# The gated delta stage's decay matrices made from broadcast rows of running sums

## The reference, cut to what matters

```python
dec = jnp.cumsum(g, axis=-1)
gam = jnp.exp(jnp.where(incl, dec[..., :, None] - dec[..., None, :], -jnp.inf))
a_low = jnp.where(strict, jnp.einsum('bhnid,bhnjd->bhnij', kb, k) * gam, 0.0)
t_inv = lax.linalg.triangular_solve(a_low + eye, ...)
qk = jnp.einsum('bhnid,bhnjd->bhnij', q, k) * gam
...
v_new = u_c - jnp.einsum('bhck,bhkv->bhcv', w_c, s)
o = jnp.einsum('bhck,bhkv->bhcv', qd_c, s) + jnp.einsum('bhcs,bhsv->bhcv', qk_c, v_new)
```

## Time and profile before

| | us |
|---|---|
| three runs: lowest, median, highest | 2285.00, 2287.24, 2290.63 |
| the profiled execution, its own time | 2291.59 |
| its span from the first to the last instruction | 2289.8 |
| PE busy / DVE / ACT / POOL in the span | 2212.5 / 1489.2 / 893.0 / 1098.7 |
| gated delta stage, from SP's first issue to the next stage's first matmul | 399.68 to 660.69 |
| start of the four trips' exps (L1128) | 406.29, 468.81, 531.69, 594.55 |

### The profile page before, as it was taken

One profiled execution on the slowest core, in us unless ns is written; L12 is line 12 of the kernel. 1 busy time (PEld: TensorE's weight loads), 2 busy tenths in 40 slices (PEclk: granted clock), 3 DMA queues, 4 the chain that ended last, 5 costly groups with the idle time before them and its releaser, 6 DMA issues.

```text
span 2289.8 us, 30456 instructions
## 1 busy us (share of the span) xinstructions
PE 2212.5 (97%) x10576; PEld 1842.1 (80%) x10576; DVE 1489.2 (65%) x3535; ACT 893.0 (39%) x1420; POOL 1098.7 (48%) x885
## 2 busy tenths in 40 slices
PE   8999868999989999999999999999999999999998
PEld 6787756888878888888888888888888888888886
DVE  4554568666654362078788888893339887878783
ACT  6454354444443333243333333342323323232343
POOL 3433134544424334426666666665427665555500
PEclk9999979999999999999999999999999999999999
DMA  4222143255233232234444444446479999999940
GB/s 171 78 89 74 40 131 107 95 192 192 92 115 129 98 132 89 88 96 142 148 142 148 138 152 145 145 143 245 149 248 342 389 375 364 343 363 345 363 168 37
DMA packets 168815, 403.12 MB, mean 176 GB/s; under 512 B 27648, under 2 KB 101632, under 8 KB 158368
## 3 DMA queue, kind: packets, MB, share of 16 engines
q1 hardware_dynamic: 133920, 334.77, 42.4%
q0 software_dynamic: 34816, 67.41, 8.0%
HBM read 336.84 MB, written 65.28 MB: 176 GB/s over the span
## 4 chain that ended last, share of the span: by engine, by line
PE 68%; DVE 1%; DMA 1%; ACT 1%; issue 0%; POOL 0%; DVEq 0%; POOLq 0%
PE ps L1434 13%; PE ps L181 11%; PE ps L183 11%; PE ps L182 11%; PE ps L2494 7%; PE ps L2495 7%; PE ps L2496 7%; PE ps L1767 1%; PE ps L2546 1%; DMA down_picked_gelu_sb<-a_dense,chosen_gelu_at_sb 0%; DMA a_dense<-up_gelu_sb 0%; POOL down_picked_gelu_sb L2226 0%; PE ps L1517 0%; PE ps L2524 0%; ACT ffn_norm_scaled_sb L1658 0%
## 5 line engine op out<-in xcount | busy, mean ns | idle before, releaser
L2015 POOL DMA_INDIRECT g_dense<-up_gates_summed_sb,up_gate_at_sb x384 | 414.8, 1080 | 259.5 <-issue 216.2
L181 PE MATMUL ps<-n_high_sb,up_u_high_sb 128*128 128x512 f32 x1024 | 398.5, 389 | 0.0
L183 PE MATMUL ps<-n_high_sb,up_u_low_sb 128*128 128x512 f32 x1024 | 398.4, 389 | 0.0
L182 PE MATMUL ps<-n_low_sb,up_u_high_sb 128*128 128x512 f32 x1024 | 398.4, 389 | 0.0
L2494 PE MATMUL ps<-down_v_high_sb,down_w_high_sb 128*128 128x512 f32 x768 | 299.0, 389 | 1.0 <-DVE down_w_low_sb L2270 1.0
L2496 PE MATMUL ps<-down_v_high_sb,down_w_low_sb 128*128 128x512 f32 x768 | 298.8, 389 | 0.0
L2495 PE MATMUL ps<-down_v_low_sb,down_w_high_sb 128*128 128x512 f32 x768 | 298.8, 389 | 0.0
L1858 DVE TENSOR_TENSOR up_u_low_sb<-up_u_sb,up_u_high_sb 128x1024 fp32r<-128x1024 f32 x128 | 156.2, 1222 | 143.7 <-ACT up_u_high_sb L2034 143.2
L2414 ACT ACTIVATE down_v_high_sb<-down_v_sb 128x1024 fp32r<-128x1024 f32 x120 | 125.8, 1048 | 308.8 <-PE ps L2496 292.0
L2236 POOL DMA_INDIRECT expert_rows_sb<-expert_v,chosen_expert_sb x128 | 155.9, 1218 | 167.1 <-DVE h_sb L2286 64.1
L2046 ACT ACTIVATE up_gelu_sb<-ps 128x512 f32<-128x512 f32 x128 | 76.5, 598 | 407.0 <-PE ps L183 406.9
(11 more groups left out here) (366 smaller groups left out, 4524.3 us busy)
## 6 DMA issues: line engine op xcount, KB each, us to landing
up_u_sb<-expert_u SPq DMA_DIRECT2D x128, 512.0 KB, 3.8
down_v_sb<-expert_v SPq DMA_DIRECT2D x32, 2048.0 KB, 11.9
a_dense<-up_gelu_sb SPq DMA_DIRECT2D x128, 256.0 KB, 2.2
g_dense<-nought_sb SPq DMA_DIRECT2D x8, 3072.0 KB, 11.2
down_gelu_sb<-a_dense SPq DMA_DIRECT2D x32, 768.0 KB, 4.7
down_gates_sb<-g_dense SPq DMA_DIRECT2D x32, 768.0 KB, 6.3
w_slots_sb<-w_conv SPq DMA_DIRECT2D x19, 1024.0 KB, 4.8
decay_rows_sb<-decay_sum_rows SPq DMA_DIRECT2D x16, 512.0 KB, 6.0
```

The costliest lines, as they stand in the source:

```text
L181: pe.matmul(out, ah, bh, start=k == 0, stop=False)
L182: pe.matmul(out, ah, bl, start=False, stop=False)
L183: last = pe.matmul(out, al, bh, start=False, stop=k == n - 1)
L2015: pool.indirect_dma_start(cells, at, summed[:, tt, k:k + 1], None).then_inc(stored[tt], 16)
```

## The change

The gated delta stage makes its decays as the SSD stage does. `project_stage` writes all 48 running sums back into `m.decay` (SSD's 32, then the gated delta heads' 8 forward and 8 backward), turns and stores 48 rows, and then makes of each pair the two numbers a token that limits and biases need. `m.sums` is gone, and `m.decay` has two spare columns of zeros. In `gdn_stage`:

- SP loads, for each unit, the rows of forward and backward sums of a head, broadcast over 128 partitions (128 x 2 x 256 fp32, 256 KB): four loads ahead of the halves, and four after every even gate piece, behind a wait for the exps that read the tile.
- DVE makes the log decays (`limits`, two operations of 128x128 a unit). Those of trip one stand ahead of the loop, those of the next trip ahead of z of unit 0. The last trip makes limits that nobody reads.
- ACT takes the exp, two of 128x128 a unit, with a sum as bias: one matrix a chunk, which serves both directions. POOL's masks read it twice.
- TensorE's sums (L1280), POOL's steps (L1181) and the tile `steps` are gone. TensorE begins a trip with the k-k and q-k products, and POOL's mask of a unit waits, besides the exp, for the unit's last output.

```diff
                     sums = m.ps[:, 5, :].rearrange("p (n t a c) -> p n t a c", n=4, t=TT, a=2)
                     for n in range(2):
-                        act.activation(m.sums[:, :, n * SSD_H:(n + 1) * SSD_H], sums[:, n, :, 0, :], ACT.Copy)
+                        act.activation(m.decay[:, :, n * SSD_H:(n + 1) * SSD_H], sums[:, n, :, 0, :], ACT.Copy)
+                        at = 2 * SSD_H + n * GDN_H
+                        act.activation(m.decay[:, :, at:at + GDN_H], sums[:, n, :, 1, n * GDN_H:(n + 1) * GDN_H], ACT.Copy)
...
                         dve.tensor_tensor(w, w, m.small[:, c:TT:TS, c * SSD_H:(c + 1) * SSD_H], ALU.mult)
                 if t == ROWS_AT + 2:
                     dve.wait_ge(rows_turned, 1)
-                    forward, backward = m.sums[:, :, 0:SSD_H], m.sums[:, :, SSD_H:2 * SSD_H]
-                    st.done(dve.tensor_tensor(backward, backward, forward, ALU.subtract))
-                    dve.tensor_scalar(forward, forward, -1.0, None, ALU.mult)
+                    for at, n in ((0, SSD_H), (2 * SSD_H, GDN_H)):
+                        forward, backward = m.decay[:, :, at:at + n], m.decay[:, :, at + n:at + 2 * n]
+                        st.done(dve.tensor_tensor(backward, backward, forward, ALU.subtract))
+                        dve.tensor_scalar(forward, forward, -1.0, None, ALU.mult)
...
+            rows = m.sum_rows[2 * SSD_H:48].rearrange("(d h) t -> h d t", d=2)
+
+            def load(i):
+                for u in U:
+                    hh, s = lanes[u]
+                    if i:
+                        sp.wait_ge(decayed[u], i)
+                    src = rows[i % TRIPS * HEADS + hh, :, s * L:(s + 1) * L].unsqueeze(0).broadcast_to([P, 2, L])
+                    sp.dma_start(sum_rows[u][:, :, :].rearrange("p (d c) n -> p d (c n)", d=2), src).then_inc(rows_in[u], 16)
+
+            load(0)
             sp.dma_start(halves[:, :, :], m.ins["halves"].rearrange("p (n c) -> p n c", c=P)).then_inc(halves_in, 16)
             sp.wait_ge(nought_made, 1)
...
+                if q % 2 == 0:
+                    load(q // 2 + 1)
                 if q < 6:
                     clear(q)
...
                 for u in U:
-                    act.wait_ge(summed[u], i + 2)
-                    act.activation(e[u][:, :, :], whole4(u), ACT.Exp).then_inc(decayed[u], 1)
+                    hh, s = lanes[u]
+                    act.wait_ge(limited[u], i + 1)
+                    for c in range(TS):
+                        sums = m.decay[:, TS * s + c, bass.ds(i * HEADS + (2 * SSD_H + hh), 1)]
+                        last = act.activation(e[u][:, c, :], backward[u][:, c, :], ACT.Exp, bias=sums)
+                    last.then_inc(decayed[u], 1)
...
-                    hh, s = lanes[u]
-                    hold(pool, m, summed[u], i + 1)
-                    for d in range(2):
-                        g = m.decay[:, TS * s:TS * s + TS, bass.ds(i * HEADS + (32 + hh + d * GDN_H), 1)].broadcast_to([P, TS, P])
-                        last = pool.tensor_tensor(steps[u][:, 2 * d:2 * d + 2, :], g, pair(sq(m, "ge" if d else "le")), ALU.mult)
-                    last.then_inc(stepped[u], 1)
-
-                for u in U:
+                    hold(pool, m, out_done[u], i + 1)
                     pool.wait_ge(decayed[u], i + 1)
-                    pool.tensor_tensor(items(qk[u]), items(e[u]), sq_pair(m, "le", 2), ALU.mult).then_inc(masked[u], 1)
+                    pool.tensor_tensor(items(qk[u]), both(e[u]).unsqueeze(1).broadcast_to([P, 2, TS, P]), sq_pair(m, "le", 2),
+                                       ALU.mult).then_inc(masked[u], 1)
...
+            def limits(i, u):
+                hh, s = lanes[u]
+                for c in range(TS):
+                    d = m.decay[:, TS * s + c, bass.ds(i * HEADS + (2 * SSD_H + GDN_H + hh), 1)]
+                    last = dve.scalar_tensor_tensor(backward[u][:, c, :], backward[u][:, c, :], d, forward[u][:, c, :],
+                                                    ALU.subtract, ALU.min)
+                last.then_inc(limited[u], 1)
+
+            for u in U:
+                dve.wait_ge(rows_in[u], 16)
+                limits(0, u)
             with dve.Fori(0, TRIPS) as i:
...
                             dve.wait_ge(split_done[w], i * 2 + 2)
+                        for w in U:
+                            dve.wait_ge(rows_in[w], i * 16 + 32)
+                            limits(i + 1, w)
                     dve.wait_ge(ks_done[u], i + 2)
...
-                pe.sem_inc(summed[u], 1)
                 pe.sem_inc(ks_done[u], 1)
             pe.sem_inc(side.filled, 1)
             with pe.Fori(0, TRIPS) as i:
                 for u in U:
+                    pe.wait_ge(staged[u], i + 1)
                     pe.wait_ge(out_done[u], i + 1)
-                    pe.wait_ge(stepped[u], i + 1)
-                    for d in range(2):
-                        last = pe.matmul(whole(u)[:, d * L:(d + 1) * L], sq(m, "lt" if d else "gt"),
-                                         steps[u][:, 2 * d:2 * d + 2, :].rearrange("p c n -> p (c n)"), start=True, stop=True)
-                    last.then_inc(summed[u], 1)
-                for u in U:
-                    pe.wait_ge(staged[u], i + 1)
-                    pe.wait_ge(decayed[u], i + 1)
```

More of the change, by code:

```diff
@@ L831, in _ @@
         def _(sp):
-            rows = m.sum_rows.rearrange("(d h) t -> d h t", d=2)
+            rows = m.sum_rows[0:2 * SSD_H].rearrange("(d h) t -> d h t", d=2)
             def load(g, s):
@@ L872, in decays @@
                         col = g * SSD_R + h
-                        last = act.activation(e[s][:, t, h, :], e[s][:, t, h, :], ACT.Exp, bias=m.sums[:, TS * s + t, col:col + 1])
+                        last = act.activation(e[s][:, t, h, :], e[s][:, t, h, :], ACT.Exp, bias=m.decay[:, TS * s + t, col:col + 1])
                 last.then_inc(decayed[s], 1)
@@ L996, in limits @@
                         forward, backward = (sum_rows[s][:, d, h, t * P:(t + 1) * P] for d in range(2))
-                        last = dve.scalar_tensor_tensor(e[s][:, t, h, :], backward, m.sums[:, TS * s + t, col:col + 1], forward,
+                        last = dve.scalar_tensor_tensor(e[s][:, t, h, :], backward, m.decay[:, TS * s + t, col:col + 1], forward,
                                                         ALU.subtract, ALU.min)
@@ L1055, in gdn_stage @@
     kq = per("kq", [P, 2, L])
-    steps, e, at, qk = (per(x, [P, 4, P]) for x in ("steps", "decay", "a_t", "qk"))
+    sum_rows, e, at, qk = (per(x, [P, 4, P]) for x in ("sum_rows", "decay", "a_t", "qk"))
+    forward, backward = [x[:, 0:2, :] for x in sum_rows], [x[:, 2:4, :] for x in sum_rows]
     vn, kd, first_part, invs = per("v_new", [P, 4, P]), per("k_dec", [P, 2, P]), per("first_part", [P, 2, P]), per("inverse_t", [P, 2, P])
```

21 lines of the change are left out of this document (11 added, 10 removed).

## The result

Five runs of each kernel on the same chip: 2303.09 us after (2299.3 to 2308.47), 2289.85 before (2285.0 to 2292.62). The ratio is 1.0055, 95% interval 1.004 to 1.0071: some 13 us slower, where +7.9 was forecast. That is beyond the 2300 at which the range ended. The kernel before had a median of 2289.85 us here, 2.6 more than the 2287.24 from which the forecast counted. The profiled execution took 2300.31 us, its span is 2298.5.

The account below looks back on a forecast made before the run. TensorE held 68% of the span, but the stage's chain ran through ACT, POOL and DVE. Load +3.7, unit start -1.1, trip's end -0.7, plus two or three falls of 2.4: middle +7.9 on 2287.2, so 2295 us, range 2284 to 2300.

Parts of the forecast that it names:

- The first trip's load: Gated delta stage's start: 1 MB of rows ahead of the gate weights delays the first split by 3.7 us, bounds 2.0 to 7.0.
- The clock: Ahead of the levels, trips two to four: 3 in 4 each that TensorE drops to half clock, 2.4 us a fall.
- Rival 1: No clock fall, or one: +1.9 to +4.3 us, 2289 to 2291.5 us, likeliest 2290; chance 0.33.
- The second unit's start: DVE's second unit starts 7.55 us behind ACT's gate split, not 7.91: 0.36 us off in trips two to four, 1.1 in all.
- Behind the trip's end: Last level to state products: 0.23 us less three times, as POOL's next-trip steps go; 0.7 us in all, bounds 0 and 1.2.
- The limits: Eight DVE operations a trip, 2.18 us, fit in DVE's 3.81 us idle before the state products: cost 0.
- rival 3: The limits do not fit under their cover: fully on the path 8.8 us, some 2298 us; chance 0.05.
- Rival 2: Removed sums were on the path: 3.6 us a trip won, 2280 us, chance 0.06; milder form 1.8, 2285 us, chance 0.06.
- The sum: Whole kernel: +1.9 us without the clock, +6.7 with two falls, +9.1 with three, middle +7.9.

Follow-up runs that it names:

- experiment 1: The changed kernel with the first trip's four 256 KB row loads issued in the stage before: ratio 1.0011 to the kernel before, stage 264.79 us.
- Experiment 4: Changed kernel, trip one's rows loaded a stage earlier, 1 MB still awaited from other sources: split at 8.8 (differing 2 KB), 10.6 (differing 1 KB), 11.3 us (repeated 2 KB).
- experiment 3: The changed kernel with the removed sums' matmuls put back as dummies nobody reads, one execution: levels 35.06, 33.67, 33.69, 33.69 us.
- experiment 2: The changed kernel with 15 of TensorE's 21 gate matmuls ahead of the levels spread between the first level's units: ratio 1.0037 to the kernel before.
- experiments 5 to 7: Edits of experiment 1 and experiment 2 together (ratio 0.9992 to before); then exponentials a trip ahead (0.9962); then those in ACT's idle time (0.995).

## Why the prediction was right and wrong

- **The first trip's load** was the step that failed most: +3.7 forecast, +7.58 measured, and 7.7 by experiment 1. The wait was the right one, its size was not. I took one rate from the difference of two stage starts (2 MB of rows less the halves) and carried it over to this load. The SSD stage's rows come in 1 KB pieces for all partitions too, so that is not where the two part; this load of 1 MB is slower all the same. Experiment 4 shows what its 7.6 us hang on (2.5 on the repeated addresses, 1.8 on the packets' size), but not why the SSD stage pays less. Even my upper bound of 7.0 was too low, and the range did not carry it in full. With 7.6 in place of 3.7 the middle of the forecast is 2299 us, and 2301.6 from the median that the kernel before had in this comparison.
- **The clock**: right in kind and direction. That the total fits (+4.96, forecast 4.8 to 7.2) is luck, as two errors stand against each other and one execution can lie anywhere from 3.7 to 9.7 (experiment 4). I gave two or three falls of 2.4 us; there were four, of 0.4 to 1.8 us. The price of a full one was right (experiment 4). Trip one, which I had counted as free, had one of 1.3 us. Rival 1, no fall or one, is refuted. The idle gaps were as short as the forecast said, up to 1.66 us, and the clock fell all the same.
- **The second unit's start**: 7.59 us behind the split for a forecast of 7.55, and 0.36 is what the sums cost (experiment 3). Yet split to first level fell only by 0.21 to 0.24 in trips two to four, as DVE met POOL's masks in L1251 as well. Trip one, counted as unchanged, lost 0.38. Of 1.1 us 0.3 came.
- **Behind the trip's end**: -0.66 for -0.7. **The limits**: hidden in every trip; rival 3 is refuted. Rival 2, the removed sums on the path, is refuted by experiment 3: putting their time back costs 0.36 us a trip, not 3.6. (What spoke for it was misread as well: two of trip two's four exps waited for L1280, not three.)
- **The sum**: stage +11.53 for +7.9 in the middle: +3.9 from the load, +0.8 from the unit's start, -1.0 from the clock against 6.0. The medians differ by 13.2, of which the interval (9 to 16 us) leaves the rest open.

## What to carry to other kernels

Work taken from TensorE where it only waits can still be paid for, because the work left over thins out ahead of a dense stretch: look at TensorE's busy time in the last few us before it, and spread filler matmuls there rather than run them in one piece. A half-clock stretch that still comes then lies where other engines cover it (levels 139.6 to 135.0 us in experiment 2, with two such stretches). A load that is hidden in all trips but the first stands in front of everything in the first; give it a place in the stage before, and don't cost it by its bytes alone, nor by the rate of another load: in this kernel 1 MB of 1 KB pieces for all partitions could be used after 7.2 us in one stage and 10.5 in the next, and packet size and repeated addresses moved the delay behind it by 4.4. And what a change frees from a dependence (here the exponentials, which no longer follow a matmul) is worth more where another engine idles than where it stood: that took 9.4 us off the stage (experiments 5 to 7), the removed work itself 0.7.

## What the runs showed of the hardware

- 1 MB of transfers ahead of others on one queue delayed them by 3.2 us (2 KB packets, differing addresses) to 7.6 us (1 KB packets, a few rows read for all 128 partitions). At another place 2 MB of 1 KB packets, rows for all 128 partitions too, ran at up to 383 GB/s.
- TensorE's granted clock fell to 0.50 behind 6.4 us with 2.40 to 4.41 us busy and no idle gap above 1.66 us, in trips two to four of all five kernels with this order. Through a gap of 2.9 us with work directly behind it, it stayed at 1.00 (experiment 2); behind the gap it stayed there in trip two and fell after 1.4 and 0.2 us in trips three and four. The levels lost 0.41 to 0.43 us for each us at 0.50.
- Eight DVE operations of 128x128 with two inputs took 2.06 us alone and 4.07 when two of them ran beside POOL's masks, 1.36 and 1.34 us each instead of 0.34.
